# Hybrid backbone on one core: gate strips ahead of turnings, square sums by token, and inverse blocks copied by two engines

## The chip, the cores and the metric

One core of one Trainium2 chip. The metric is the device time of one execution in microseconds (us); the runs of the kernel before are three, with their median. TensorE is called PE below, VectorE DVE, ScalarE ACT, GpSimd POOL, and SyncE SP, as the profile does. "Granted clock" is the share of PE's full clock that it was given in a stretch: 1.00 is 2.4 GHz, 0.50 is 1.2 GHz.

## The reference, cut to what matters

Two layers over 256 latent tokens and 256 context tokens, 1024 channels, all float32. In each layer three branches (a short convolution, a two-directional recurrence over tokens, windowed attention) start from one modulated norm and are merged under sigmoid gates; a convolutional FFN follows. The context tokens are not needed after the last layer, so that the second layer computes only half of the token columns in most places.

```python
def rmsnorm(x, g):
    return x * lax.rsqrt(jnp.mean(x * x, axis=-1, keepdims=True) + NORM_EPS) * g

def modulate(x, g, shift, scale):
    return rmsnorm(x, g) * (1.0 + scale) + shift

def trunk_layer(xc, xl, c, c_ctx, cos, sin, p, ctx_out):
    hl, hc = modulate(xl, norm1_g, ...), modulate(xc, norm1_g, ...)
    # columns of h @ w_in: B, C, x of the convolution; r, k, v; three low-rank inputs; q, k, v; three gates
    att = windowed_attention(rope(q) * ATT_SCALE, rope(k), v, kc, vc, sink)   # context: context_attention
    # recurrence, forward and backward in t, 16 heads of 64:
    #   S = S * w_t + (S a_t) b_t^T + v_t k_t^T ;  y_t = S r_t
    rwkv = ((group_norm(y) * ln_g + ln_b) + bonus) * g
    conv = B * dwconv3(C * x, conv_w)
    m = sig(ga) * (conv @ a_out_w) + sig(gb) * (rwkv @ rwkv_out_w) + sig(gc) * (att @ attn_out_w)
    xl = xl + mod[2] * (m @ w_o)
    xl = xl + mod[5] * conv_ffn(modulate(xl, norm2_g, mod[3], mod[4]), p)
# the end: rmsnorm(xl, final_norm_g)
```

## The kernel before, in words

The activations lie with channels on the 128 partitions and the 512 tokens (256 context, 256 latent) along the free axis: xT and hT are 8 tiles of 128x512. Weights come in strips of 8 x 128x128 (512 KB) through a ring of 5 buffers that SP loads in the order in which PE uses them; a buffer comes free with the first matmul of the next strip. A strip is 8 matmuls of 512 columns (256 in the second layer where only the latent tokens count) into one PSUM bank; each of them is two entries of the trace, so that a strip is x16.

Every engine runs a stream of its own, written out by hand in program order, and waits on semaphores. PSUM is dealt out by three rings of two: A (banks 0, 1, small products that ACT copies out), G (6, 7, dense strips) and Q (pairs from 2 and 4, evacuated by DVE for the most part). `take` waits until the ring's next bank is free.

**The start** (`begin`): x and ctx are transposed on PE (L541), DVE copies them into xT (L1654) and squares them (L1605); 8 matmuls with a matrix of ones (`square_sum`, L486) sum the squares over channels and give every partition the sum of each token; ACT takes Ln and Exp (L1247, L1249), DVE multiplies (L1611). Beside that the modulation vectors come from four units of `ada_w` of 2 MB each (L496, copied by ACT at L1263, picked by PE at L518), and with them ACT modulates hT (L1257) for the first strips (L472). The same `square_sum` stands at the end of `merged_out` and of `ffn` in both layers: five norms, 8 matmuls each.

**Mixing** (`mix`, first loop over i, 8 passes per layer): one pass handles two heads, i.e. 128 channels. Its small matrix work stands between fillings: `fill(steps, n)` issues dense matmuls of the next pass's strips (order r, k, C, x, v, B) worth n halves of 256 columns. The order on PE in a pass is: `diagonal_blocks` (L606), `turn_hats`, `turn_values`, `pair_products`, a fill, `half_step` (L656, waits for DVE's chain from `turn_blocks` to `spread_blocks`, L1854 to L1914), `corners`, `below_left`, `value_products`, `corner_below`, `bonus_sums`, then for the next pass `key_sums` and `decays` (L590, L593), then `through_inverse` (L724, four blocks lrb0 to lrb3 from ring A, which ACT copies at L1392 after its own `decays`, L1325 and L1331), then the chain of 8 chunks `state_in` (L741) and `state_out` (L755) with a fill after each, and `outputs` (L773, L780). `state_out(0)` waits for `first_ready`, which DVE gives with `state_in(0)` (L1937). Between the chunks DVE computes the next pass's hats in small steps (L1762 to L1805); the fifth step (L1785) needs the exponentials that ACT makes in `powers` (L1339). ACT's copy of C is L1400 (`conv_gate`); the bank after it in ring G is wanted by the x strip.

**Attention** (`attend`, 8 steps t): scores on PE, maxima on DVE, exponentials on ACT, shares on DVE, then PE transposes the probabilities (`turn_probs`, L849), ACT copies them (L1447, L1450), and PE multiplies with the values (`weighted`, L861, copied at L1455). The gates and the output strips of the first two branches (`gate`, `branch`) are spread between. In the first layer a group of modulation columns is computed too (`ada_group` L506, `ada_pick` L518). All small products take ring A.

## Time and profile before

| | |
|---|---|
| runs | 3131.89, 3135.42, 3133.84 us; median 3133.84 |
| profiled execution | 3132.01 us, of which the span is 3130.2 |
| mean granted clock of PE | 0.973 |
| busy in the span | PE 2926.4, PE weight load 1763.4, DVE 1267.4, ACT 749.0, POOL 51.5 us |
| DMA | 264 MB, mean 84 GB/s |

The stretches of the span: start 0 to 75 us, mixing of the first layer to about 865, its attention to about 1290, the merge and FFN to about 1930, mixing of the second layer to about 2560, its attention, merge and FFN to the end. A row of a timeline gives start, duration, engine, line and operation, and in brackets how long the engine had been idle before it and who released it. Entries of PE overlap a little, so starts are what to compare.

### The profile page before, as it was taken

What the parts mean: (1) busy time and instruction counts of PE and PEld (TensorE: products, weight loads), DVE (VectorE), ACT (ScalarE), POOL (GpSimd) and SP (SyncE); (2) the same over time, 40 slices, a digit from 0 to 9 for tenths busy, and PEclk for the clock granted to TensorE, in tenths of its full rate; (3) what the DMA queues carried; (4) which work ended last, traced back from release to release, by engine and by line L of the source; (5) the groups of instructions that cost most, each with busy time, mean ns of one, the idle gap of its engine ahead of it and who ended that gap; (6) DMA issues with size and microseconds to landing.
All of it is one profiled execution on the core that took longest, in us unless ns stands there. A gap on an engine that the chain in (4) does not pass through costs nothing.

```text
span 3130.2 us, 57225 instructions
## 1 busy us (share of the span) xinstructions
PE 2926.4 (93%) x25233; PEld 1763.4 (56%) x25233; DVE 1267.4 (40%) x2564; ACT 749.0 (24%) x1456; POOL 51.5 (2%) x77
## 2 busy tenths in 40 slices
PE   7899999999989988999999999888998899999999
PEld 3455555555644444444444444555666667788887
DVE  2555555555222222112444211555666643322541
ACT  2233333233222112101111001323344422221110
POOL 1000000000000000000000000000000000000000
PEclk9999999999999998999999999989999999999999
DMA  7212222221324223322222223322211114344553
GB/s 232 71 42 65 71 58 65 72 65 50 82 74 106 77 78 91 88 74 66 78 74 81 69 74 102 85 64 72 72 52 45 45 44 122 108 115 129 158 150 115
DMA packets 499846, 264.26 MB, mean 84 GB/s; under 512 B 42848, under 2 KB 493744, under 8 KB 499088
## 3 DMA queue, kind: packets, MB, share of 16 engines
q1 hardware_dynamic: 497872, 251.57, 28.4%
q0 software_dynamic: 1728, 9.03, 0.8%
q8 instruction: 201, 3.29, 0.4%
q14 instruction: 45, 0.37, 0.0%
HBM read 255.31 MB, written 5.24 MB: 83 GB/s over the span
## 4 chain that ended last, share of the span: by engine, by line
PE 87%; ACT 6%; DVE 3%; issue 2%; DMA 2%; SPq 0%; DVEq 0%; ACTq 0%
PE psum L451 56%; PE psum L1018 7%; PE psum L472 2%; PE psum L638 2%; DMA strips<-in_w_in_dram 1%; PE psum L724 1%; PE psum L741 1%; ACT arena L1325 1%; PE psum L755 1%; PE psum L706 1%; PE psum L791 1%; PE psum L839 1%; PE psum L486 1%; PE psum L861 1%; PE psum L518 1%
## 5 line engine op out<-in xcount | busy, mean ns | idle before, releaser
L451 PE MATMUL psum<-hT,strips 128*128 128x512 f32 (+1 forms) x3968 | 1471.1, 520 | 48.6 <-ACT arena L1400 27.6
L451 PEld LDWEIGHTS psum<-hT,strips 128*128 128x128 f32 x3968 | 742.7, 194 | 576.9 <-issue 485.8
L1018 PE MATMUL psum<-arena,strips 128*128 128x512 f32 (+1 forms) x704 | 229.4, 486 | 0.0
L1018 PEld LDWEIGHTS psum<-arena,strips 128*128 128x128 f32 x704 | 133.7, 190 | 92.8 <-issue 83.5
L451 PE MATMUL psum<-arena,strips 128*128 128x512 f32 (+1 forms) x512 | 169.6, 486 | 3.0 <-DVE done L2058 3.0
L451 PEld LDWEIGHTS psum<-arena,strips 128*128 128x128 f32 x512 | 97.1, 190 | 71.5 <-issue 60.7
L2023 DVE SCALAR_TENSOR_TENSOR arena<-arena,psum 128x512 f32<-128x512 f32 (+1 forms) x32 | 17.7, 554 | 292.8 <-PE psum L451 292.8
L1556 ACT COPY arena<-psum 128x512 f32<-128x512 f32 (+1 forms) x88 | 42.1, 479 | 390.2 <-PE psum L451 375.4
L1673 DVE TENSOR_SCALAR arena<-arena 128x512 f32<-128x512 f32 (+1 forms) x88 | 37.0, 421 | 240.3 <-ACT arena L1556 240.1
L1835 DVE TENSOR_TENSOR arena<-psum,tables 128x1024 f32<-128x1024 f32 x48 | 58.5, 1220 | 110.3 <-PE psum L638 110.3
L724 PE MATMUL psum<-arena 64*64 64x128 f32 (+1 forms) x1024 | 67.8, 283 | 29.8 <-ACT arena L1331 25.5
L2171 DVE SCALAR_TENSOR_TENSOR arena<-psum,mod,arena 128x256 f32<-128x256 f32 x24 | 10.9, 481 | 208.6 <-PE psum L1018 208.6
L1435 ACT ACTIVATE arena<-psum,arena 128x512 f32<-128x512 f32 (+1 forms) x96 | 58.1, 613 | 149.1 <-DVE arena L1998 148.6
L1941 DVE TENSOR_TENSOR arena<-psum,arena 64x256 f32<-64x256 f32 x112 | 47.3, 422 | 109.9 <-PE psum L741 109.8
L1247 ACT ACTIVATE arena<-psum,tables 128x512 f32<-128x512 f32 (+1 forms) x5 | 3.0, 602 | 367.9 <-PE psum L486 367.9
L472 PE MATMUL psum<-hT,strips 128*128 128x512 f32 (+1 forms) x160 | 73.9, 626 | 16.4 <-ACT hT L1257 16.4
L451 PE MATMUL psum<-conv_branch,strips 128*128 128x512 f32 (+1 forms) x256 | 86.4, 490 | 1.9 <-ACT arena L1462 1.6
L1462 ACT ACTIVATE arena<-psum 128x512 f32<-128x512 f32 (+1 forms) x48 | 23.7, 495 | 267.4 <-PE psum L451 267.4
L451 PE MATMUL psum<-rwkv_branch,strips 128*128 128x512 f32 (+1 forms) x256 | 85.2, 486 | 0.0
L724 PEld LDWEIGHTS psum<-arena 64*64 64x64 f32 x1024 | 56.5, 146 | 45.3 <-ACT arena L1331 28.1
L638 PE MATMUL psum<-arena 64*128 64x128 f32 (+1 forms) x1024 | 75.3, 290 | 6.9 <-issue 6.9
L741 PEld LDWEIGHTS psum<-arena 64*64 64x64 f32 x896 | 35.0, 134 | 67.3 <-issue 49.0
(240 smaller groups left out, 3318.2 us busy)
## 6 DMA issues: line engine op xcount, KB each, us to landing
strips<-in_w_in_dram SPq DMA_DIRECT2D x158, 512.0 KB, 4.2
strips<-in_ffn_up_dram SPq DMA_DIRECT2D x88, 512.0 KB, 3.8
strips<-in_ada_w_dram SPq DMA_DIRECT2D x80, 512.0 KB, 3.8
strips<-in_ffn_down_dram SPq DMA_DIRECT2D x32, 512.0 KB, 4.0
arena<-in_ada_w_dram SPq DMA_DIRECT2D x4, 2048.0 KB, 15.3
strips<-in_w_in_dram SPq DMA_DIRECT2D x32, 256.0 KB, 3.8
strips<-in_a_out_w_dram SPq DMA_DIRECT2D x16, 512.0 KB, 4.5
strips<-in_rwkv_out_w_dram SPq DMA_DIRECT2D x16, 512.0 KB, 5.8
```

The source lines that it names most:

```text
L451: ins = mm(s.o[:, first:T], strip[:, b, k, :], rhs[:, k, first:T], k == 0, k == KT - 1)
L472: ins = mm(ss[j].o[:, first:T], strip[:, bs[j], k, :], hT[:, k, first:T], k == 0, k == KT - 1)
L486: ins = mm(s.o[:, lo:T], ones[:, :], sq[:, k, lo:T], k == 0, k == KT - 1)
L638: ins = one(PS[:, b0 + h, (c % 4) * n:(c % 4 + 1) * n], BK[d][rows(h), c].rearrange("p j t -> p (j t)"), ar[d][rows(h), c, 0:n // CH].rear ...
L724: ins = one(PS[r, BANK_A[s.b], q * n:(q + 1) * n].rearrange("p (k t) -> p k t", t=CH), TLR[r, 8 * h + 4 * d + m].rearrange("p b t -> p (b ...
L741: ins = one(PS[r, BANK_P[s.b] + h, d * CH:(d + 1) * CH], AR[i % 2][d][rows(h), c, 0, :], GG[rows(h), c, d, :])
L1018: ins = mm(s.o[:, lo:T], strip[:, b, j, :], hid[:, k, lo:T], k == 0, k == FT - 1)
L1435: ins = act.activation(pr[u][:, x:x + 2 * T // g], PS[:, b0 + x // T, x % T:x % T + 2 * T // g], ACT.Exp, bias=st[:, u, 1, i:i + 1], accum ...
L1556: act.copy(upp[:, b, lo // SEG:, 1:SEG + 1], s.o[:, lo:T].rearrange("p (s t) -> p s t", t=SEG)).then_inc(s.free, 1)
L1673: ts(dst, src[:, :, 1:n + 1], g1, None, MUL).then_inc(s_vec, 1)
L1835: tt(EE[:, 0:2, j, d].rearrange("p k h c t -> p k (h c) t").rearrange("p k q t -> p q k t"), o, mask.unsqueeze(1).broadcast_to([P, 8, 2, C ...
L1941: tt(dst, o, add, ADD).then_inc(s.free, 1)
```

## The change

- `gate(0, t)` goes ahead of `turn_probs(t, 2)`, and `gate(1, t)` ahead of `turn_probs(t, 0)`, on PE and ACT; `ada_pick` of attention goes behind `branch(0, t)`.
- For the first norm ACT squares the rows of x token by token with an accumulated sum, takes Ln and Exp on 4 columns, DVE spreads each over 128 columns, and PE turns these 4 tiles (`spread_tokens`). For the four others DVE adds the first 7 squares up and PE multiplies two tiles with the ones instead of 8.
- In mixing, DVE copies lrb0 and lrb1, placed between its `bonus` and its `decays`, ACT only lrb2 and lrb3. ACT's `conv_gate(i + 1)` goes ahead of its `through_inverse`. PE fills 4 (2 in the second layer) between `decays(i + 1)` and `through_inverse`, and a little less between the chunks. `diagonal_blocks(i + 1)` goes ahead of `outputs(i)`. `ada_pick` goes behind a fill. DVE's `conv_taps` goes ahead of its last `state_in`.

```diff
-            def square_sum(n, k, lo):
+            def square_sum(n, lo, last):
-                if k == 0:
+                if not last:
                     take(A, "norm", n)
                 s = slots["norm", n]
-                pe.wait_ge(ev["sq_ready"], KT * n + k + 1)
-                ins = mm(s.o[:, lo:T], ones[:, :], sq[:, k, lo:T], k == 0, k == KT - 1)
-                if k == KT - 1:
+                pe.wait_ge(ev["sq_ready"], 2 * n + last - 1)
+                ins = mm(s.o[:, lo:T], ones[:, :], sq[:, KT - 1 if last else 0, lo:T], not last, last)
+                if last:
                     ins.then_inc(s.full[0], 1)
+            def spread_tokens():
+                pe.wait_ge(ev["rows_ready"], 1)
+                s = take(A, "norm", 0)
+                for j in range(4):
+                    ins = one(s.o[:, j * P:(j + 1) * P], rs_rows[:, j, :], tab["ident"])
+                ins.then_inc(s.full[0], 1)
...
                         if t > 0:
                             weighted(t - 1, 1)
+                        gate(0, t)
                         if lo == 0:
                             turn_probs(t, 2)
-                        if t > 0 and ATT_ADA[l][t - 1]:
-                            ada_pick(A, *ATT_ADA[l][t - 1], part_att)
-                        gate(0, t)
...
                         branch(0, t)
+                        if t > 0 and ATT_ADA[l][t - 1]:
+                            ada_pick(A, *ATT_ADA[l][t - 1], part_att)
                         scores(t, 1)
                         if lo == 0:
                             weighted(t, 0)
+                        gate(1, t)
                         turn_probs(t, 0)
-                        gate(1, t)
...
                 fill(steps, everything)
+                diagonal_blocks(0)
                 for i in range(KT):
                     ahead = i < KT - 1
                     steps = dense(i + 1) if ahead else attention_dense()
-                    diagonal_blocks(i)
...
                     half_step(i)
+                    pair_products(1, 0, i)
+                    fill(steps, 10 if wide else 6)
                     if MIX_ADA[l][i]:
                         ada_pick(A, *MIX_ADA[l][i], part_mix)
-                    pair_products(1, 0, i)
-                    fill(steps, 10 if wide else 6)
...
                         decays(i + 1)
+                        fill(steps, 4 if wide else 2)
                     through_inverse(i, ahead)
...
-                            fill(steps, 4 if wide else 2.4)
+                            fill(steps, 3.8 if wide else 2.3)
...
                     fill(steps, everything)
+                    if ahead:
+                        diagonal_blocks(i + 1)
                     outputs(i)
```

ACT: the start, and a pass of mixing.

```diff
-                norm(0, 0)
+                act.wait_ge(s_x, 64)
+                for j in range(4):
+                    ins = act.activation(hT[:, 2 * j:2 * j + 2, :].rearrange("p k t -> p (k t)"), xin[:, j, :], ACT.Square,
+                                         accum_out=token_rs[:, j:j + 1])
+                ins.then_inc(s_act, 1)
+                act.wait_ge(*order.next())
+                act.activation(token_rs, token_rs, ACT.Ln, bias=tab["eps_norm"], scale=1.0 / D).then_inc(s_act, 1)
+                act.wait_ge(*order.next())
+                act.activation(token_rs, token_rs, ACT.Exp, scale=-0.5).then_inc(ev["token_ready"], 1)
+                s = await_slot("norm", 0)
+                act.copy(rs, s.o).then_inc(ev["rs_ready"], 1)
...
                 def through_inverse(i):
-                    for m in range(4):
+                    for m in range(2, 4):
...
                         decays(i + 1)
+                        conv_gate(i + 1)
                     through_inverse(i)
                     if ahead:
                         powers(0, i + 1)
-                        conv_gate(i + 1)
                         powers(1, i + 1)
```

DVE: the squares, the start, and a pass of mixing.

```diff
             def square(k, lo):
-                tt(sq[:, k, lo:T], xT[:, k, lo:T], xT[:, k, lo:T], MUL).then_inc(ev["sq_ready"], 1)
+                ins = tt(sq[:, k, lo:T], xT[:, k, lo:T], xT[:, k, lo:T], MUL)
+                if k == KT - 1:
+                    ins.then_inc(ev["sq_ready"], 1)
+                elif k > 0:
+                    ins.then_inc(s_vec, 1)
+                    dve.wait_ge(*order.next())
+                    ins = tt(sq[:, 0, lo:T], sq[:, 0, lo:T], sq[:, k, lo:T], ADD)
...
+                dve.wait_ge(ev["token_ready"], 1)
+                for j in range(4):
+                    ins = ts(rs_rows[:, j, :], ones[:, :], token_rs[:, j:j + 1], None, MUL)
+                ins.then_inc(ev["rows_ready"], 1)
...
+                def through_inverse(i):
+                    for m in range(2):
+                        s = filled(f"lrb{m}", i)
+                        k0 = 1 if 2 * m >= c0 else 2
+                        n = (3 - k0) * 4 * CH
+                        for p in range(2):
+                            r = rows(p)
+                            ins = dve.tensor_copy(EE[r, k0:3, m // 2, :, :, 2 * (m % 2) + p].rearrange("p k d h t -> p k (d h) t").rearrange("p k q t -> p q k t"),
+                                                  PS[r, BANK_A[s.b], 0:n].rearrange("p (q k t) -> p q k t", q=4, t=CH))
+                        ins.then_inc(s.free, 1)
...
                     bonus(i)
+                    through_inverse(i)
                     if ahead:
                         decays(i + 1)
...
+                        if ahead and c == NCH - 2:
+                            t = conv_taps(i + 1)
                     if ahead:
-                        t = conv_taps(i + 1)
```

## Rows read from the trace of the kernel before

**Rows 1.** The page: busy time by engine (us, share, instructions), and the chain.

```profile
PE 2926.4 (93%) x25233; PEld 1763.4 (56%) x25233; DVE 1267.4 (40%) x2564; ACT 749.0 (24%) x1456; POOL 51.5 (2%) x77
...
PE 87%; ACT 6%; DVE 3%; issue 2%; DMA 2%; SPq 0%; DVEq 0%; ACTq 0%
```

**Rows 2.** PE's waits from 880 to 1330 us: total us, times, longest.

```profile
PE psum L849 <- ACT arena L1455: 19.9, 8, 2.5
PE psum L518 <- ACT arena L1447: 12.8, 7, 3.0
...
PE psum L849 <- DVE arena L2011: 3.0, 2, 1.5
```

**Rows 3.** Timeline of PE in the first layer's attention, t = 2 to 3.

```profile
1024.11 1.02 PE L518 MATMUL psum<-tables,arena 128*128 128x2 f32 x8 [1.35 <-ACT arena L1447]
1025.00 8.81 PE L451 MATMUL psum<-hT,strips 128*128 128x512 f32 x16
...
1047.27 7.03 PE L451 MATMUL psum<-hT,strips 128*128 128x512 f32 x16
```

**Rows 4.** Windows: length, busy by engine, granted clock, DMA share, GB/s.

```profile
860.00:1290.00 430.00, 384.22 (x1704) 187.08 (x1703) 99.05 (x244) 87.42 (x245) 0.00 (x0) 0.96 0.32 86
```

**Rows 5.** Timeline of PE in the first layer's mixing, pass 3.

```profile
452.13 2.14 PE L724 MATMUL psum<-arena 64*64 64x128 f32 x32 [1.51 <-ACT arena L1331]
...
455.52 0.45 PE L755 MATMUL psum<-arena 128*64 128x64 f32 x8
...
460.85 1.98 PE L451 MATMUL psum<-hT,strips 128*128 128x512 f32 x4 [0.29 <-ACT arena L1400]
```

**Rows 6.** Timeline of DVE in the same pass.

```profile
437.99 0.68 DVE L1924 COPY arena<-psum 32x512 f32<-32x512 f32 x1 [3.67 <-PE psum L683]
...
450.48 0.69 DVE L1749 TENSOR_SCALAR arena<-arena 128x1024 f32<-128x1024 f32 x1 [5.70 <-ACT arena L1325]
...
452.25 2.33 DVE L1754 TENSOR_TENSOR_SCAN arena<-tables,arena 128x512 f32<-128x512 f32 x2
454.50 0.26 DVE L1937 COPY arena<-arena 64x256 f32<-64x256 f32 x1
...
458.77 0.69 DVE L1785 SCALAR_TENSOR_TENSOR arena<-arena 128x512 f32<-128x512 f32 x1
```

**Rows 7.** Timeline of ACT in the same pass.

```profile
451.95 4.89 ACT L1392 COPY arena<-psum 64x512 f32<-64x512 f32 x8
456.86 0.64 ACT L1339 ACTIVATE arena<-arena 128x512 f32<-128x512 f32 x1
...
460.21 0.58 ACT L1400 COPY arena<-psum 128x512 f32<-128x512 f32 x1 [1.96 <-PE psum L451]
```

**Rows 8.** Timeline of PE in the second layer's mixing, pass 5.

```profile
2400.28 1.29 PE L656 MATMUL psum<-arena 32*32 32x32 f32 x128 [1.49 <-DVE arena L1914]
...
2426.20 2.62 PE L724 MATMUL psum<-arena 64*64 64x64 f32 x48 [2.13 <-ACT arena L1331]
...
2432.20 0.70 PE L451 MATMUL psum<-hT,strips 128*128 128x256 f32 x2 [1.59 <-ACT arena L1400]
```

**Rows 9.** Line L486, all its instructions: min/median/max ns, first and last start.

```profile
L486 PE MATMUL psum<-hT,ones x80: 379/592/697, 21.2 to 3119.7; 128*128 128x512 f32 x48, 128*128 128x256 f32 x32
```

**Rows 10.** Timeline of PE and DVE at the start.

```profile
12.30 4.38 PE L541 MATMUL psum<-tables,arena 128*128 128x128 f32 x24 [5.39 <-DMA arena<-in_x_dram]
...
15.57 1.29 DVE L1605 TENSOR_TENSOR hT<-arena 128x512 f32<-128x512 f32 x2
...
21.18 7.13 PE L486 MATMUL psum<-hT,ones 128*128 128x512 f32 x16
...
39.56 11.98 PE L472 MATMUL psum<-hT,strips 128*128 128x512 f32 x24 [1.74 <-ACT hT L1257]
```

**Rows 11.** Line L1088, the loads of the four ada units.

```profile
L1088 SPq DMA_DIRECT2D arena<-in_ada_w_dram x4: 639/1646/3748, 4.2 to 27.6; - x4
...
DMA to landing us min/median/max: 10.6/15.3/20.9
```

More of the change, by code:

```diff
@@ L544, in begin @@
                 turn_params(0)
-                for k in range(KT):
-                    square_sum(0, k, 0)
+                spread_tokens()
                 pe.wait_ge(ev["c_ready"], 1)
@@ L987, in mix @@
                         if c > 0:
-                            fill(steps, 4 if wide else 2.4)
+                            fill(steps, 3.8 if wide else 2.3)
                         if c < NCH - 1:
                             state_out(c, i)
-                            fill(steps, 4 if wide else 2.4)
+                            fill(steps, 3.8 if wide else 2.3)
                     fill(steps, everything)
+                    if ahead:
+                        diagonal_blocks(i + 1)
                     outputs(i)
@@ L1194, in load_params @@
                 if l == 0:
-                    pool.memset(ones[:, :], 1.0)
                     for m in range(DEPTH):
@@ L1477, in attend @@
                         exps(t, 0)
+                        gate(0, t)
                         if lo == 0:
@@ L1481, in attend @@
                             ada_raw(*ATT_ADA[l][t - 1])
-                        gate(0, t)
                         exps(t, 1)
@@ L1485, in attend @@
                             weighted(t, 0)
+                        gate(1, t)
                         probs(t, 0)
-                        gate(1, t)
                         if ATT_ADA[l][t]:
@@ L1604, in square @@
             def square(k, lo):
-                tt(sq[:, k, lo:T], xT[:, k, lo:T], xT[:, k, lo:T], MUL).then_inc(ev["sq_ready"], 1)
+                ins = tt(sq[:, k, lo:T], xT[:, k, lo:T], xT[:, k, lo:T], MUL)
[5 more added lines that the diff above has]
+                    ins = tt(sq[:, 0, lo:T], sq[:, 0, lo:T], sq[:, k, lo:T], ADD)
+                    if k == KT - 2:
+                        ins.then_inc(ev["sq_ready"], 1)
+                    else:
+                        ins.then_inc(s_vec, 1)
+                        dve.wait_ge(*order.next())
             def scaled(n, lo):
@@ L1644, in begin @@
             def begin():
+                dve.memset(ones[:, :], 1.0).then_inc(s_vec, 1)
+                dve.wait_ge(*order.next())
                 s = await_slot("c")
@@ L1654, in begin @@
                     dve.tensor_copy(xT[:, 2 * u:2 * u + 2, :], PS[:, BANK_P[s.b]:BANK_P[s.b] + 2, :]).then_inc(s.free, 1)
-                    dve.wait_ge(*s.freed)
-                    for k in range(2 * u, 2 * u + 2):
-                        square(k, 0)
+                dve.wait_ge(ev["token_ready"], 1)
+                for j in range(4):
+                    ins = ts(rs_rows[:, j, :], ones[:, :], token_rs[:, j:j + 1], None, MUL)
+                ins.then_inc(ev["rows_ready"], 1)
                 setup(0)
```

17 lines of the change are left out of this document (9 added, 8 removed).

## The prediction, made before the changed kernel was run

> **What bounds the kernel now.** I read the page first: PE is busy 93% of the span and is 87% of the chain that ended last [rows 1]. So time is won where PE stands idle, where its clock is low, or where it has less to do; work moved from ACT to DVE wins nothing by itself. Then I asked for PE's waits stretch by stretch, since the average hides that they differ. In the first layer's attention 35.7 us are waits for small copies and shares, in three kinds [rows 2]: 19.9 in 8 (one per step, the second half of `turn_probs(t, 0)` waits until ACT has come to a copy queued behind exponentials), 12.8 in 7 (`ada_pick` behind `turn_probs(t, 2)`), 3.0 in 2. The same stretch shows a granted clock of 0.96, that is 0.04 x 430 = 17 us lost [rows 4]. The strip behind such a wait shows the second loss: 8.81 us, where the same strip without it takes 7.03 [rows 3]; each fall of the clock costs about 1.8 us. Then I read one pass of mixing in each layer on PE, DVE and ACT side by side [rows 5 to 8]. The first layer's passes are nearly full: 1.51 and 0.29 us of waits in a pass of some 91. The second layer's have 2.13, 1.59 and, in the passes without an ada group, 1.49.
>
> **Attention.** Before each of the two turnings there now stands a gate strip, 7.0 us of PE work [rows 3] that needs nothing but its weights. The wait of 2.49 goes: ACT's queued copies take about 1.5 us. `ada_pick` has a whole `branch` strip between it and the turning. The ring sees the same order of strips. All 35.7 us go. For waits that go the clock stays up: I take 14 of the 17 us, since waits for strips behind each ada group stay. Next late there is nothing that I can find: the copy of the gate is hidden by the turning that follows it. Sum: -50. Bounds: -36 if the clock keeps falling for the waits that stay, -53 at most. In the second layer these turnings show no waits; 0.
>
> **Square sums.** 80 entries are 40 matmuls [rows 9]. The 16 entries of one wide norm take 7.13 us [rows 10], so 0.86 us a matmul after the overlap, half of it with 256 columns. Four norms lose 6 matmuls each: 2 x 6 x 0.86 + 2 x 6 x 0.43 = 15.5 us, all on PE between strips. DVE gets 6 additions per norm of about 0.65 us (the squares: 1.29 for two [rows 10]) while PE's next strip takes 7.0 (or 3.5): hidden. The end of a norm is as long as before: then too, two products stood behind the last strip. Sum: -15.5; bounds -12 (if a wait takes part of it) and -16.
>
> **The start.** x is there at 12.3 us [rows 10]. ACT squares 4 tiles of 128x1024; 512 columns cost it about 0.6 [rows 7], so 1.1 each: 16.8. Ln, a table load and Exp on 4 columns: about 19.8 at most with two table loads of some 1.3. DVE, freed of its squares, has xT by 19.5; 4 small spreads, PE's four turnings, ACT's copy: rs at about 22, where before the sums alone end at 28.3 [rows 10]. Then another bound takes over: the units of `ada_w`. The second one, issued near 5, lands 20.9 us later [rows 11], at 25.9; its product, copy and pick, and the first modulated tile, took 32.7 to 39.6 before, some 6.9 us that start at 25.9 now. So the first strip starts near 32.6 in place of 39.6 [rows 10]: -7. Bounds: -10 (this stretch ran in part at the low clock) and -3 (the low clock lies across more of it). The second half of the start keeps its order, and its loads have time. ones on DVE costs 0.2 us before anything is due.
>
> **Mixing, first layer.** Here I expect a loss. Before, DVE starts `decays` at 450.48, as soon as ACT has given it data, and gives `first_ready` at 454.8 (0.69, 0.69, 2.33 and 0.26 us [rows 6]), a little before PE comes to `state_out(0)` at 455.52 [rows 5]. Now two copies per block stand ahead of `decays` in DVE's queue, and they wait for PE. In this pass's times: PE ends `decays` at 449.5 (lrb1 starts at 452.13 behind a wait of 1.51 and lrb0's 1.1 [rows 5]), fills 1.95 us (half of the x16 strip's half), and does lrb0 from 451.5 to 452.5 and lrb1 to 453.6; the wait of 1.51 is gone. DVE copies two halves of lrb0 and two of lrb1 at 0.65 each: 452.6 to 455.2; lrb2 and lrb3 wait 0.35 and 0.3 for these and end at 456.3. `decays` then takes DVE to 458.8, `state_in(0)` to 459.1. PE stands idle 459.1 - 456.3 = 2.8 us. Behind PE's wait is everything, since `state_out(0)` is next in its queue and no fill is ahead of it. The second wait is on ACT: 22 matmuls of fill are issued before `through_inverse`, and C is complete with the 24th. So `conv_gate`, now first, waits for the fill behind `state_out(0)`, 2.35 us after its start; then it takes 0.6, two blocks take 4.89 / 2 = 2.4 [rows 7], and the first `powers` 1.4 (456.86 to 458.3). They are ready 6.8 us after `state_out(0)` starts; before, they were ready ahead of DVE's fifth step at 458.77 [rows 6]. DVE stands there, with `state_out(1)` behind it in its queue, and PE reaches `state_in(2)` 1.5 us before that is done. The wait of the x strip for C (0.29) stays. Idle per pass: 0.65 + 2.8 + 1.5 + 0.3 = 5.2, against 2.0 before (with 0.2 at lrb3): +3.2 a pass, 7 passes, +22. A stall of 2.8 us within a few us of others lets the clock fall in perhaps half of the passes, 1.8 each less what it costs there now: +5. Sum +27. Bounds: +8 (DVE's copies at the rate of its small 64-row copy of 0.26, ACT ahead) and +38 (a clock fall in each pass). Earlier `diagonal_blocks` bring DVE's chain forward by the outputs, 3.8 us, but `half_step` does not wait for it in this layer in most passes: 0. Its cover if DVE were later: the fill of 7 us ahead of it. The moved `ada_pick` is hidden both ways.
>
> **Who should copy from PSUM** is a point where the Trainium skill speaks against this change. DVE's copy of 512 columns from PSUM is 0.68 to 0.70 [rows 6], ACT's 4.89 / 8 = 0.61 [rows 7]. The Trainium skill (VectorE: DVE Perf Modes, Specifications) puts it that ScalarE sits closer to PSUM and VectorE closer to SBUF; the rows agree, by 0.08 us a copy. By that alone the change would cost 4 x 0.08 = 0.3 us a pass at the one place where DVE is late. In my sum it is not the rate but the place in DVE's queue that costs.
>
> **Mixing, second layer.** The same steps with blocks half as large: the fill is 2 halves, which completes C, so that `conv_gate` does not wait and the 1.59 goes. lrb1 still waits 1.1 for ACT's copy of g in place of 2.13 [rows 8]. PE has lrb1 at 2426.9, DVE's two copies of it (about 0.4 each with 256 columns) end at 2427.75, `decays` and `state_in(0)` need the 3.8 us of [rows 6]: 2431.5. PE, waiting 0.3 for lrb1's bank, is done with lrb3 at 2429.1: 2.4 of idle. 3.5 in place of 4.0 us: -0.5 a pass. `half_step`'s 1.49 [rows 8] shrinks only by 0.65, since DVE's chain, brought forward by 2 us, meets `masked_pairs`, whose products PE makes no earlier; this for four passes. With the last pass of each layer, where two engines share the copies and nothing else is late (-1 each): -3.5 - 2.6 - 2 = -8. I keep 3 of it back for the clock: -5. Bounds -15 and +10, by whether the stall of 2.4 brings the clock down.
>
> **The sum** against the profiled execution: 3132.0 - 50 - 15.5 - 7 + 27 - 5 = 3081.5; its time is 1.8 below the median of the runs, so 3083.
>
> **Rivals.**
> (a) The mixing doesn't lose: DVE's place is covered, because `first_ready` was given earlier than I think or the copies are short. For it: DVE was idle 5.70 us ahead of `decays` [rows 6]. Against it: it was idle before PE has lrb0. Mixing 0 in place of +27: 3056.
> (b) The mixing loses more: a clock fall in every pass of both layers and `state_in` late more than once per pass. +27 becomes +40, -5 becomes +10: 3111.
> (c) The gates only move the wait: if a gate strip is not there in time, PE waits for its load where it waited for a copy. The ring is emptied by four ada strips in 2 us, and PE waits for strips already. If half of attention's gain goes so: 3108.
> (d) Slower than before: DVE never catches up in the chain of chunks. A pass has 7 links from DVE to PE; if each came late, at 1 us a link, 14 passes are +98 on top of the rest, 3180. It decides from where DVE's work between two links exceeds PE's time for them, 4.7 us in the first layer (two fills of 1.98 and two small products) and 3.3 in the second. DVE's is about 3.8 in both while hats are computed, for four of the seven links, so that in the second layer it is close.
>
> **Chances.** My sum 0.48; (a) 0.20; (b) 0.17; (c) 0.11; (d) 0.04. The forecast is that of the likeliest, 3083. Its own range by the bounds is 3068 to 3098; to hold 8 in 10 it must take in most of (a) and of (b) and (c): 3054 to 3110. A measurement of this kernel can tell about 0.2%, 6 us, from no change. Within it lies only what is between (b) and (d), 0.02; slower 0.03; faster 0.95.
>
> **What would show it.** Right: in attention no wait at L849 and L518, waits for strips unchanged, a clock near 0.99; L486 with 16 entries in the four later norms; the first strip near 32.6 with the wait ahead of it on the second unit. In the first layer's mixing a wait of `state_out(0)` near 2.8 for DVE's `first_ready`, one of `state_in(2)` near 1.5, none for g. Wrong: `state_out(0)` without a wait would take the +27 away; waits at each chunk in the second layer would mean (d).

## The result, and the profile after

The changed kernel takes 3108.8 us (median of 4 runs, 3100.3 to 3118.2) against 3132.9 of the kernel before (4 runs): ratio 0.9922, 95% interval 0.9894 to 0.995. It is faster by 24 us, where 50 were forecast. The time lies in the range, but the gain is less than half of the forecast, and most of the reason is in one stage.

The page of the profiled execution (span 3116.4 us, the slowest of the four runs) answers to [rows 1]; it shows next to nothing, 18 us less of PE's work and 44 us more of DVE's:

```profile
PE 2908.8 (93%) x25177; PEld 1757.7 (56%) x25177; DVE 1311.2 (42%) x2649; ACT 724.3 (23%) x1401; POOL 51.6 (2%) x76
```

So the span has to be cut by stage. The marks are events that both traces have: the first dense strip, ACT's square of the last pass in mixing, ACT's Ln in each norm. Lengths in us, of one profiled execution each:

| stage | before | after | difference | forecast |
|---|---|---|---|---|
| start, to the first dense strip | 73.8 | 65.1 | -8.7 | -7 |
| mixing, first layer | 776.3 | 834.2 | **+57.9** | +27 |
| attention and merge, first layer | 604.9 | 542.2 | **-62.7** | -55 |
| FFN, first layer | 469.8 | 465.2 | -4.6 | -5 |
| mixing, second layer | 683.7 | 692.0 | +8.3 | -5 |
| attention and merge, second layer | 274.1 | 272.3 | -1.8 | -2.6 |
| FFN, second layer, and end | 247.6 | 245.3 | -2.3 | -2.6 |

The differences sum to -13.8 us and not to -24, because the profiled execution of the changed kernel is the slowest of its four. Its granted clock is 0.970 over a span of 3116.4 us; the fastest has 0.975 and 3098.5 us, and 0.005 x 3116 is some 16 of the 18 us between them. So the same kernel varies by that much through the clock alone, and a stage rich in clock falls, as mixing is, can hold several us of it.

The windows of the two changed stages, before and after (columns as in [rows 4]). Before:

```profile
73.80:850.10 776.30, 733.02 (x10057) 426.25 (x10055) 414.31 (x739) 249.66 (x410) 16.27 (x18) 0.98 0.23 62
850.10:1455.10 605.00, 557.42 (x2111) 262.96 (x2110) 125.88 (x295) 100.37 (x270) 3.12 (x7) 0.97 0.31 86
```

After:

```profile
65.10:899.30 834.20, 753.97 (x10057) 437.53 (x10055) 435.17 (x771) 231.86 (x378) 16.57 (x18) 0.95 0.21 58
899.30:1441.60 542.30, 530.71 (x2098) 254.87 (x2098) 130.12 (x301) 99.56 (x270) 3.12 (x7) 1.00 0.35 95
```

Both stages moved in idle time and in clock. Mixing has the same 10057 entries of PE as before, but is busy 754 us with them instead of 733, at a clock of 0.95 instead of 0.98, and idle 80 instead of 43. Attention is idle 12 us instead of 48, at a clock of 1.00.

PE's waits in attention of the first layer: of [rows 2] none is left. The largest is that of the strips behind the ada groups (8.4 us in 6 before); beside it stand only two single waits of 1.7 and 0.8 us:

```profile
PE psum L453 <- DMA strips<-in_w_in_dram: 8.8, 6, 2.5
```

PE's waits in the first layer's mixing (line, whom it waited for: total us, times, longest), after:

```profile
PE psum L764 <- DVE arena L1983: 18.6, 7, 2.7
PE psum L680 <- issue: 9.6, 4, 2.8
PE psum L453 <- DVE arena L1847: 8.8, 7, 1.3
PE psum L750 <- DVE arena L1998: 8.6, 7, 1.4
PE psum L453 <- ACT arena L1420: 8.2, 5, 7.1
PE psum L733 <- DVE arena L1973: 7.6, 16, 0.6
PE psum L624 <- ACT arena L1432: 4.1, 7, 0.6
```

Line numbers have moved: L764 is `state_out`, L1983 the copy that gives `first_ready`, L750 `state_in`, L733 `through_inverse` and L1973 DVE's copies in it, L453 a dense strip, L1847 `gated`, L624 `turn_hats`, L1432 ACT's copy of y. The wait of 1.51 for g at [rows 5] is gone from this list. The 7.1 in the fifth line is in the prologue and stood there before.

The same pass as in [rows 5 to 7], after. PE:

```profile
460.20 1.88 PE L453 MATMUL psum<-hT,strips 128*128 128x512 f32 x4
462.01 1.97 PE L733 MATMUL psum<-arena 64*64 64x128 f32 x32
464.60 1.09 PE L733 MATMUL psum<-arena 64*64 64x128 f32 x16 [0.61 <-DVE arena L1973]
466.02 1.09 PE L733 MATMUL psum<-arena 64*64 64x128 f32 x16 [0.33 <-DVE arena L1973]
469.77 0.69 PE L764 MATMUL psum<-arena 128*64 128x64 f32 x8 [2.66 <-DVE arena L1983]
470.39 3.78 PE L453 MATMUL psum<-hT,strips 128*128 128x512 f32 x4
```

DVE:

```profile
463.15 2.81 DVE L1973 COPY arena<-psum 64x512 f32<-64x512 f32 x4 [7.60 <-PE psum L733]
466.00 0.69 DVE L1784 TENSOR_SCALAR arena<-arena 128x1024 f32<-128x1024 f32 x1
466.61 0.69 DVE L1786 TENSOR_SCALAR arena<-arena 128x1024 f32<-128x1024 f32 x1
467.21 2.33 DVE L1789 TENSOR_TENSOR_SCAN arena<-tables,arena 128x512 f32<-128x512 f32 x2
469.46 0.26 DVE L1983 COPY arena<-arena 64x256 f32<-64x256 f32 x1
...
478.51 0.69 DVE L1820 SCALAR_TENSOR_TENSOR arena<-arena 128x512 f32<-128x512 f32 x1 [3.24 <-ACT arena L1362]
```

Read it downwards. DVE stands idle for 7.60 us. In the last 1.9 us of them the input of its `decays` is there (ACT's L1345, L1325 before, starts at 459.96, and DVE could follow 1.28 us later, as it did before), but its copies come first in its queue and wait for PE. Then copies, `decays` and the copy for `first_ready` run without a gap from 463.15 to 469.7, and PE waits for the last of them. The strip behind takes 3.78 us for four entries that take 1.98 elsewhere; the clock there is half. Two windows of 2 us behind the stall (466 to 468 still shows 1.00; in this pass the clock falls at 469.2, 0.6 us before the stall ends):

```profile
470.00:472.00 2.00, 2.00 (x10) 1.11 (x9) 1.90 (x5) 0.00 (x0) 0.00 (x0) 0.50 0.00 0
472.00:474.00 2.00, 2.00 (x3) 0.34 (x1) 0.54 (x1) 0.00 (x0) 0.00 (x0) 0.50 0.00 0
```

### The profile page after: what moved, and what is told of

It reads as the page before. It is cut to its first block, busy times and chain, and to the rows that moved or that the text cites. A ratio compares the mean times of both kernels' runs of the same rounds, so it can differ in the third digit from the quotient of the medians.

```text
span 3116.4 us, 57161 instructions
## 1 busy us (share of the span) xinstructions
PE 2908.8 (93%) x25177; PEld 1757.7 (56%) x25177; DVE 1311.2 (42%) x2649; ACT 724.3 (23%) x1401; POOL 51.6 (2%) x76
## 4 chain that ended last, share of the span: by engine, by line
PE 87%; DVE 5%; ACT 4%; issue 2%; DMA 2%; SPq 0%; DVEq 0%; ACTq 0%
PE psum L453 55%; PE psum L1028 7%; PE psum L474 2%; PE psum L647 2%; DMA strips<-in_w_in_dram 1%; PE psum L750 1%; PE psum L764 1%; PE psum L870 1%; DVE arena L1789 1%; PE psum L848 1%; PE psum L800 1%; PE psum L715 1%; PE psum L637 1%; PE psum L858 1%; DVE arena L1973 1%
## 5 line engine op out<-in xcount | busy, mean ns | idle before, releaser
L453 PE MATMUL psum<-hT,strips 128*128 128x512 f32 (+1 forms) x3968 | 1483.3, 523 | 46.4 <-DMA strips<-in_w_in_dram 20.5
L453 PEld LDWEIGHTS psum<-hT,strips 128*128 128x128 f32 x3968 | 747.0, 195 | 580.5 <-issue 491.5
L453 PE MATMUL psum<-arena,strips 128*128 128x512 f32 (+1 forms) x512 | 167.9, 486 | 3.0 <-DVE done L2104 3.0
L453 PEld LDWEIGHTS psum<-arena,strips 128*128 128x128 f32 x512 | 97.1, 190 | 71.5 <-issue 60.7
L764 PEld LDWEIGHTS psum<-arena 128*64 128x64 f32 x896 | 35.7, 138 | 102.4 <-DVE arena L1983 40.6
L764 PE MATMUL psum<-arena 128*64 128x64 f32 x896 | 51.4, 237 | 37.3 <-DVE arena L1983 37.3
L453 PE MATMUL psum<-conv_branch,strips 128*128 128x512 f32 (+1 forms) x256 | 85.8, 488 | 0.3
L453 PE MATMUL psum<-rwkv_branch,strips 128*128 128x512 f32 (+1 forms) x256 | 85.2, 486 | 0.0
L750 PEld LDWEIGHTS psum<-arena 64*64 64x64 f32 x896 | 36.8, 140 | 82.2 <-issue 42.5
L1973 DVE COPY arena<-psum 64x512 f32<-64x512 f32 (+1 forms) x64 | 35.5, 555 | 101.9 <-PE psum L733 101.2
```

The lines of the kernel that those rows point to most:

```text
L453: ins = mm(s.o[:, first:T], strip[:, b, k, :], rhs[:, k, first:T], k == 0, k == KT - 1)
L750: ins = one(PS[r, BANK_P[s.b] + h, d * CH:(d + 1) * CH], AR[i % 2][d][rows(h), c, 0, :], GG[rows(h), c, d, :])
L764: ins = one(PS[rows(h), BANK_P[s.b], d * CH:(d + 1) * CH], EE[:, 2, c // 4, d, h, c % 4, :], RV[:, c, d, h, :])
L1973: ins = dve.tensor_copy(EE[r, k0:3, m // 2, :, :, 2 * (m % 2) + p].rearrange("p k d h t -> p k (d h) t").rearrange("p k q t -> p q k t"), ...
```

## The experiments

All ratios are to the kernel before, run beside the kernel in question on the same chip. It took 3132.9 us beside the changed kernel, 3134.5 beside e1 to e4, 3129.8 beside e5 to e8 and 3129.1 beside e9 to e12; across these groups the ratios compare better than the times. The two stages are those of one profiled execution each.

| kernel | us | ratio, 95% interval | mixing, first layer | mixing, second layer |
|---|---|---|---|---|
| changed kernel | 3108.8 | 0.9922, 0.9894 to 0.9950 | 834.2 | 692.0 |
| e1 mixing as before | 3057.4 | 0.9751, 0.9733 to 0.9768 | 777.4 | 684.7 |
| e2 ACT copies all | 3066.8 | 0.9782, 0.9768 to 0.9797 | 787.4 | 686.0 |
| e3 DVE copies behind decays | 3101.3 | 0.9891, 0.9876 to 0.9906 | 821.5 | 687.5 |
| e4 diagonal behind outputs | 3102.1 | 0.9891, 0.9874 to 0.9908 | 824.8 | 691.9 |
| e5 e2, gated early | 3063.5 | 0.9782, 0.9760 to 0.9804 | 779.3 | 688.9 |
| e6 DVE copies the last two | 3068.4 | 0.9801, 0.9783 to 0.9819 | 783.8 | 688.6 |
| e7 C copy at old place | 3093.2 | 0.9879, 0.9855 to 0.9902 | 816.7 | 683.0 |
| e8 e5, diagonal late | 3050.3 | 0.9745, 0.9721 to 0.9768 | 773.3 | 686.3 |
| e9 fill behind the blocks | 3084.4 | 0.9855, 0.9839 to 0.9871 | 811.2 | 680.8 |
| e10 gates alone | 3070.4 | 0.9810, 0.9793 to 0.9827 | 776.2 | 683.1 |
| e11 sums and start alone | 3119.7 | 0.9965, 0.9947 to 0.9983 | 782.1 | 680.0 |
| e12 e1 with DVE's copies | 3106.8 | 0.9926, 0.9907 to 0.9945 | 811.3 | 702.8 |

The second layer's mixing differs by up to 5 us between kernels whose code there is the same (before, e1, e10, e11: 680.0 to 684.7), the first layer's by 6. Differences of that size in one column say nothing.

**e1: everything but mixing.**

```diff
@@ the changed kernel, all edits of mixing undone @@
-                        fill(steps, 4 if wide else 2)
...
-                    if ahead:
-                        diagonal_blocks(i + 1)
...
-                    for m in range(2, 4):
+                    for m in range(4):
...
-                    through_inverse(i)
                     if ahead:
                         decays(i + 1)
```

> The changed kernel with all six edits of mixing undone (copies, place of the C copy, fills, diagonal blocks, the pick, conv_taps); the gates, the square sums and the start stay changed. Theory: by stages of the two traces, mixing costs the change 57.9 us in the first layer and 8.3 in the second, and everything else gives 80. So this kernel should stand at 3133 - 80 = 3053 us, with the first layer's attention as short as in the changed kernel (542 against 605 us to the next norm). Rival: attention is short only because mixing hands over its buffers in another state, and its gain goes with mixing: 3090 or above.

3057.4 us (some 3053 expected), attention and merge of the first layer 542.9. The rival falls: all of the loss is in mixing, and it takes 50 us from a kernel that has 77 to give.

**e2: ACT copies all four blocks.**

```diff
-                    for m in range(2, 4):
+                    for m in range(4):
...
-                        conv_gate(i + 1)
                     through_inverse(i)
                     if ahead:
                         powers(0, i + 1)
+                        conv_gate(i + 1)
...
-                    through_inverse(i)
                     if ahead:
                         decays(i + 1)
```

> The changed kernel with all four inverse blocks copied by ACT and the C copy at its old place (ahead of the copies it would wait for itself); the fill ahead of through_inverse, the early diagonal blocks, the pick and conv_taps stay. Theory A (DVE's place in its queue): the waits for first_ready (2.66 each, 14) and for state_in(2) (up to 1.4) and for DVE's copies vanish and with them two clock falls of 1.7 per pass of the first layer: 7 passes x 8 = 56 and some 20 in the second layer, and the wait for g (1.5, 2.1) stays gone by the fill: near 3035. Theory B (too many small products in a row, diagonal blocks beside outputs, starve PE of instructions and pull the clock down): most of the loss stays: near 3080.

3066.8: the copies, with the C copy that goes with them, are 42 us, most of the loss, but not all; theory B falls as the main cause, and theory A was too generous. PE's waits in the first layer's mixing now:

```profile
PE psum L453 <- ACT arena L1420: 11.7, 8, 7.1
PE psum L680 <- issue: 10.0, 4, 3.0
PE psum L453 <- DVE arena L1847: 8.8, 7, 1.3
PE psum L624 <- ACT arena L1432: 4.1, 7, 0.6
```

The waits for `first_ready`, for `state_in(2)` and for g are gone. Two are left that the kernel before does not have and that the prediction's sum (the "blind sum" of the expectations) does not have either: 8.8 us in 7 of a strip for DVE's `gated`, and 4.1 in 7 of `turn_hats` for ACT's copy of y. In the second layer a strip waits for C, 18.6 us in 7, where the kernel before had 11.2 in 7, since ACT comes to it later:

```profile
PE psum L453 <- ACT arena L1420: 18.6, 7, 2.7
```

**e3: the copies behind decays.**

```diff
                     bonus(i)
-                    through_inverse(i)
                     if ahead:
                         decays(i + 1)
+                    through_inverse(i)
```

> The changed kernel with DVE's two copies behind its decays instead of ahead of them. Theory A (what costs is that decays and first_ready wait behind copies that wait for PE): DVE does decays while PE fills, copies lrb0 and lrb1 at about +2 us of where they are now; lrb2 and lrb3 wait 2 us in all, but state_out(0) waits little: 1 to 1.5 us less per pass and fewer clock falls in it: 3085 to 3095. If the place does not matter, only the number of copies on DVE: 3109, unchanged.

3101.3, outside of what theory A gave by 6. It is 7.5 below the changed kernel, with intervals that overlap; the profiled stage is shorter by 12.7. The wait moves from L764 to L733, which now shows 20.8 us in 12, up to 2.7 each, in the first layer. At the head of the pass DVE's queue has no good place: either the copies hold `decays`, or `decays` holds the copies, and PE needs both before `state_out(0)`.

**e4: the diagonal blocks back at the head of the pass.**

```diff
-                    if ahead:
-                        diagonal_blocks(i + 1)
                     outputs(i)
```

> The changed kernel with the diagonal blocks back at the head of the pass, behind the outputs. Theory A: they cover ACT's copy of y again (0.8 us a pass in the first layer, 0.2 in the second), but DVE's chain starts 2 to 4 us later, so that half_step waits 0.5 longer in the second layer: within 6 us of 3109. Theory B (small products in a row): some 20 us faster, 3089, with the waits of PE that nothing explains (issue) back to half.

3102.1, 6.7 below the changed kernel, with intervals that overlap. The wait of `turn_hats` for y is gone (4.1 us), `half_step` in the second layer waits 5.2 instead of 2.9, and the waits that nothing explains are nearly as long as in the changed kernel (20.0 us in the first layer, where it has 21.7). Theory B has no case in this layer's waits; a small gain is left that the runs cannot separate from none.

**e5: gated earlier.**

```diff
-                            if ahead:
-                                gated(i + 1)
...
+                        if ahead and c == 4:
+                            gated(i + 1)
```

> As e2 (ACT copies all four blocks), and DVE's product for the x strip (gated) is placed behind its state_out(4) instead of behind state_in(5). Theory: the new wait of a dense strip for that product (8.8 us in 7, first layer) comes from the fill drawn ahead of through_inverse, which brings the B strip two matmuls forward; with gated early it vanishes, and a clock fall in each pass with it: 9 to 20 us less than e2's 3067, i.e. 3047 to 3058. Rival: the strip's place is not the cause of e2's remaining loss against e1 (10 us), which lies in the diagonal blocks: 3064 or more.

The wait of 8.8 us is gone from the list, as expected, and the first layer's mixing is shorter by 8.1. But 3063.5 is outside the 3047 to 3058 that were expected, and the ratio is e2's, 0.9782, so over the whole kernel the gain is not shown; the stage loses as much to the clock as e2's (22 us, where e2 has 20), so that the second half of the theory, a clock fall saved in each pass, does not hold; the second layer was 3 us longer in this profile.

**e6: DVE copies two blocks, but the last two.**

```diff
-                    for m in range(2):
+                    for m in range(2, 4):
...
-                    through_inverse(i)
                     if ahead:
                         decays(i + 1)
...
                             state_out(c, i)
+                            if c == 0:
+                                through_inverse(i)
```

> DVE still copies two of the four inverse blocks, but the last two (lrb2, lrb3), and behind its state_out(0); ACT copies the first two; the C copy is back at its old place. Theory (the place in DVE's queue costs, not the copying itself): decays and first_ready are not held up, the chain needs these blocks only at chunk 4, so the waits for first_ready vanish and the time is near e2's, 3067, at most 1.4 us a pass in the first layer above it: 3060 to 3080. Rival (DVE has no room for 2.5 us more in any place of the pass): 3095 to 3110, with waits of PE for state_in or state_out at the first chunks.

3068.4: the same number of copies on the same engine, and 38 us less than the changed kernel by the ratios; of these the place of the C copy accounts for some 14 (e7), so that against e7, which has it at the same place and ran beside it, 25 are left. The first layer's waits for `first_ready` are 2.1 us in all:

```profile
PE psum L764 <- DVE arena L1987: 2.1, 7, 0.3
```

So it is not the number of copies on DVE that costs. e6 changes two things at once, the place in the queue and which blocks DVE copies, and both belong to the gain: lrb2 and lrb3 are needed late, while lrb0 and lrb1 hold the banks that lrb2 and lrb3 wait for. With lrb0 and lrb1 behind `decays` little was won (e3). In the second layer, where a chunk is shorter, even this place is late: `state_out(1)` waits 2.4 in each of 7 passes for DVE's `state_in`, 16.9 us.

**e7: ACT's copy of C at its old place.**

```diff
                         decays(i + 1)
-                        conv_gate(i + 1)
                     through_inverse(i)
                     if ahead:
                         powers(0, i + 1)
+                        conv_gate(i + 1)
```

> The changed kernel with only ACT's copy of C back behind the first powers. Theory: the wait of state_in(2) (1.2 to 1.4 us in 7 passes of the first layer, 8.6 in all) comes from ACT holding its block copies and powers behind an unfinished C; it vanishes here, but in the second layer the x strip may wait for C again: 3096 to 3104 against 3109. Rival: state_in(2) is late because DVE's decays are late: the wait stays, 3109.

3093.2, 16 below the changed kernel (14 by the ratios, whose intervals just overlap) and 3 below what was expected; in the profiles the first layer's mixing is 17.5 us shorter. The wait of `state_in(2)` is gone from the list (8.6 us in 7), that of `first_ready` is unchanged:

```profile
PE psum L764 <- DVE arena L1983: 18.6, 7, 2.7
PE psum L680 <- issue: 9.9, 4, 3.1
PE psum L453 <- DVE arena L1847: 8.8, 7, 1.3
```

**e8: what is best of it.**

```diff
@@ e5, and @@
-                    if ahead:
-                        diagonal_blocks(i + 1)
                     outputs(i)
```

(The pick is back ahead of its fill as well.)

> As e5, with the diagonal blocks back behind outputs and the pick back: what is left of the change in mixing is the fill ahead of through_inverse, conv_taps and the early gated. Theory: the fill hides the wait for g (10.6 us in the first layer, 14.9 in the second before), the diagonal blocks are worth what half_step waits in the second layer less what turn_hats waits for y: within 6 us of e5, and below e1's 3057: 3035 to 3055. Rival: the clock takes back what waits give: 3057, as e1.

3050.3, the fastest of all: 13 us below e5 measured beside it, with intervals that just touch, and not to be told from e1 by its ratio. The fill ahead of the blocks takes the wait for g away (10.6 us in e1's first layer), and mixing is 773.3 where e1 has 777.4. In the second layer the wait for C is 18.6 us in 7, as in e2. Whether it is faster than e1 is not settled.

**e9: the fill where the stall is.**

```diff
-                        fill(steps, 4 if wide else 2)
                     through_inverse(i, ahead)
+                    if ahead:
+                        fill(steps, 4 if wide else 2)
```

> The changed kernel with the new fill (4, or 2 in the second layer) behind PE's through_inverse, directly ahead of state_out(0), instead of ahead of through_inverse. The wait for g (1.5) comes back and the wait of 2.66 for first_ready shrinks by the 1.95 us of fill, to about 0.9: the sum of waits in a pass stays within 0.5 us. Theory: the long stall is what lets the clock fall there (two falls of 1.7 in a pass behind it), so that cutting it in two short waits gives back 1.7 or more per pass of the first layer: 3085 to 3098. Rival: the clock follows the sum of idle time: 3105 to 3110.

3084.4, 24 below the changed kernel (21 by the ratios, whose intervals are apart). One pass, PE:

```profile
455.51 1.96 PE L733 MATMUL psum<-arena 64*64 64x128 f32 x32 [1.51 <-ACT arena L1352]
458.09 1.09 PE L733 MATMUL psum<-arena 64*64 64x128 f32 x16 [0.62 <-DVE arena L1974]
459.11 1.98 PE L453 MATMUL psum<-hT,strips 128*128 128x512 f32 x4
461.84 0.45 PE L764 MATMUL psum<-arena 128*64 128x64 f32 x8 [0.75 <-DVE arena L1984]
462.23 1.98 PE L453 MATMUL psum<-hT,strips 128*128 128x512 f32 x4
```

and the stage:

```profile
67.20:878.40 811.20, 737.52 (x10057) 429.23 (x10056) 435.08 (x771) 231.87 (x378) 16.28 (x18) 0.98 0.22 60
```

The waits of the pass are 1.51, 0.62 and 0.75 where the changed kernel has 0.61, 0.33 and 2.66: 0.7 us less, 5 in the stage. But PE is busy 737.5 us with the same 10057 entries, 16.5 less than in the changed kernel, at a clock of 0.98 instead of 0.95, and the strip behind `state_out(0)` takes 1.98. None of the falls of this stage lies behind `state_out(0)`. So the one long stall cost the fall of the clock there, and nearly the same waiting in pieces did not. How much of the 16.5 us is the stall's is less sure, since the changed kernel's profile is of its slowest run; the comparison over all kernels below does not hang on it.

**e10: the gates alone**, on the kernel before (on ACT in the same way, and the other gate too).

```diff
+                        gate(0, t)
                         if lo == 0:
                             turn_probs(t, 2)
-                        if t > 0 and ATT_ADA[l][t - 1]:
-                            ada_pick(A, *ATT_ADA[l][t - 1], part_att)
-                        gate(0, t)
```

> The kernel before with only the order of attention changed (gates ahead of the turnings, ada_pick behind the branch). From the stages: first layer's attention with its merge was 604.9 us and is 542.2, of which 5 are square sums: -57 to -58, so 3076. My blind sum had -50, 3083.

3070.4, ratio 0.981: 59 us, the stage 544.7 against 604.9. The waits of [rows 2] are gone here too, and the waits for strips are 7.1 us in 6.

**e11: sums and start alone**, on the kernel before.

```diff
-                for k in range(KT):
-                    square_sum(0, k, 0)
+                spread_tokens()
...
-                square_sum(2 * l + 2, KT - 1, lo)
+                square_sum(2 * l + 2, lo, False)
+                square_sum(2 * l + 2, lo, True)
```

> The kernel before with only the square sums and the start changed. Blind sum -15.5 and -7: 3110. From the stages: start -6 to -10, the four norms -5, -4.6, -1.8 and -2.3 = -14: 3108 to 3114.

3119.7, ratio 0.9965: 5 to 17 us, where the prediction's sum had 22.5 and the stages led me to expect some 20. The stages that hold little else show the forecast gains: start 67.0 (-6.8), FFN of the first layer 463.9 (-5.9), attention and merge of the second 271.9 (-2.2). The first layer's mixing and attention, whose code is unchanged up to the five sums, were 5.8 and 3.0 longer in this profile, the latter at a clock of 0.96. So the gain is there by stage, and over the whole kernel some 9 us of it are not seen in these runs, most of them within what two equal stages differ by.

**e12: the copies alone**, on e1.

```diff
-                    for m in range(4):
+                    for m in range(2, 4):
...
                     bonus(i)
+                    through_inverse(i)
                     if ahead:
                         decays(i + 1)
```

> The kernel e1 (gates, sums and start changed, mixing as before) with one edit of mixing added: DVE copies the first two inverse blocks, ahead of its decays. No fill, no early C, no early diagonal blocks. Theory: first_ready comes 2.7 to 2.9 us late in each of 14 passes beside the wait for g, which stays, and the clock falls behind it: waits +3.1 and clock +1.7 to +3.4 a pass in the first layer, some +1 to +3 in the second: 3057 + 34 to 50, i.e. 3090 to 3107. Rival: the copies cost only together with the other edits, which take their cover: 3057 to 3070.

3106.8 against e1's 3057.4 (ratios 0.9926 and 0.9751): this one edit costs 49 us by the times, 55 by the ratios, by itself. PE's waits in the first layer's mixing:

```profile
PE psum L764 <- DVE arena L1980: 18.6, 7, 2.7
PE psum L733 <- ACT arena L1348: 10.6, 7, 1.5
```

The first layer's stall is the same 2.66 to the hundredth, with and without fill, early C and early diagonal blocks. In the second layer it is 14.1 us in 7, and the stage is longest there, 702.8. The other edits of mixing, put on top of this one, make the changed kernel as a whole neither better nor worse than e12. By stage they cost in the first layer (834.2 against 811.3), where the fill wins 10.6 us at g and 21.5 are lost at `state_in(2)`, at `gated` and at y, and give some of it back in the second (692.0 against 702.8).

## Why the prediction was right and wrong, step by step

**What bounds the kernel: right.** Nearly every gain and loss is PE's idle time or PE's clock; the rest is the work of the square sums that PE no longer does, and 5 us in attention that are open. ACT gave 25 us of work away, and no gain of its own came of it.

**Attention: right, 8 short.** -58 without the sums (and -59 in e10) against -50, beyond my bound of -53. The waits went whole: 36 of the 58 are idle time (605.0 - 557.4 before, 542.3 - 530.7 after). The clock term was 3 too small: I kept back 3 of 17 us for the waits for strips that stay, but those (8.8 us) let it fall once; the stage now shows 1.00, and 17 us fewer are lost to the clock. The other 5 are busy time that neither the sums nor the granted clock explains; e10, which has no other edit, shows the same 5. What they are is open.

**Square sums: right by stage.** The four later norms have 16 entries in all, where they had 64 [rows 9], and the stages that hold little beside them lost 4.6, 1.8 and 2.3 us, where 5, 2.6 and 2.6 were forecast. In e11 alone the whole kernel gained less than the sum.

**Start: the number right, the bound wrong.** -8.7, in other profiles -6 to -9 (-10 in e8), against -7. The first modulated strip starts at 32.07, where 32.6 was forecast. But the bound that I named, the second unit's load, is not seen: PE was never waiting for it. The product of the first unit took 3.32 us from 21.65, at the low clock, and that with copy and pick brought PE to the second unit at 26.64, 0.7 us behind my landing time. From there to the strip it took 5.4 us and not 6.9, since the low clock now lay on the first unit's product and no longer on the second's (1.92 us, where it took 3.38 before). The two errors cancel, so part of this hit is luck.

**Mixing, first layer: the step that failed.** The mechanism was right and so were its terms one by one, in the row's own numbers: `first_ready` 2.66 (forecast 2.8), `state_in(2)` 1.2 to 1.4 (1.5), the blocks 0.94 (0.65), g gone. DVE's four copies took 2.81 us, 0.70 each, where the estimate was 0.65; ACT's take 0.59 here, so that the remark on the two engines stands, though of the rows it named for DVE only the 0.68 reads PSUM. The steps that failed are the clock term, taken at 5 us, and two waits that the sum put at nothing. What was missing, 31 us:

- The clock, 21 us more of busy time where I had 5. I took a fall in half of the passes, from the attention rows, where I had seen a stall of 2.49 without a fall and one of 1.35 with it. Not every stall of 2.49 is harmless: in the kernel before, three of the eight are followed by a fall, and four of the five of 1.35. That is seven of thirteen, so that half was fair for attention; it did not carry over to mixing. Two of the 2.49, the first with a slow strip behind it, the second with the strip of 7.03 us at 1047.27 in [rows 3]:

```profile
881.03 0.66 PE L849 MATMUL psum<-tables,arena 128*128 128x128 f32 x4 [2.49 <-ACT arena L1455]
881.52 8.73 PE L451 MATMUL psum<-hT,strips 128*128 128x512 f32 x16
...
1046.77 0.66 PE L849 MATMUL psum<-tables,arena 128*128 128x128 f32 x4 [2.49 <-ACT arena L1455]
```

  The stall of 2.66 with 0.94 ahead of it brings the clock down in six of the seven passes, in two of them for twice as long (3.4 us at half the clock, or 6.8), which makes 13.6 us; in e4, e7 and e12, with the same stall, it does so in 18 of 21. The whole stage loses 39 us to the clock, where it lost 15 before; the other 10 of this growth lie elsewhere in the passes, and why is open. That the stall is the cause is shown by e9, and by all kernels together: the five whose first layer has a stall of 2.7 us in each pass, at `state_out(0)` or at the blocks ahead of it (the changed kernel, e3, e4, e7, e12), have a granted clock of 0.95 to 0.96 in this stage, the nine others 0.97 to 0.98.
- `gated`, 8.8 us: the fill drawn ahead of the blocks brings the B strip two matmuls forward, and its bank is given free by `gated`, which DVE does only behind `state_in(5)`. I followed C through the moved fill and not the strips behind it. Shown by e5, where the wait is gone.
- ACT's copy of y, 4.1 us: the diagonal blocks stood between `outputs` and `turn_hats` and covered it. I asked what the moved blocks wait for, and not what they had hidden. Shown by e4 and e8, where it is gone.
- About 5 us more of waits that the profile calls issue; what they come from is open.

**Mixing, second layer: the waits right, the sum wrong**, +8.3 for -5. `first_ready` 2.66 (2.4), g 1.27 (1.1), C gone (as said), `half_step` 2.9 us in 3 passes for 4.3 in 3. The stall of 2.66 costs 18.6 us and the other three changes (g, C, `half_step`) give 18.6 back; on top, what is idle in all grew by 3 and busy time, i.e. clock, by 5. Part of it may be nothing: kernels with the same code here differ by 5 us.

**The rivals.** (b), a clock fall in every pass, is what happened, for the first layer as a mechanism: it had 0.17. Its second half, `state_in` late more than once per pass, did not happen. That its 3111 is so near the 3108.8 is luck: it gave mixing +50 where the profiles have +66, and the other stages won more than forecast. (a) is refuted by the wait of 2.66 itself and by e12, (c) by the strips' waits, (d) too: DVE catches up after `state_in(2)`, and in the changed kernel no later chunk waits. I weighed (b) too low: I priced it as a matter of chance per stall, from stalls of other kinds in another stage.

## What to carry to other kernels

In an engine's in-order queue a moved piece costs by where it stands: two blocks on DVE cost some 50 us ahead of `decays`, where their copies wait for PE and hold up what PE needs next, and almost nothing where DVE took the two that are needed last and copied them behind the first chunk. When work is drawn ahead or moved, follow every bank and buffer that it advances, and ask of the moved work what it had covered. Put independent dense work where the stall is, not somewhere near it: the same fill behind the blocks instead of ahead of them was worth 21 to 24 us. And a rate of clock falls that was read in one stage did not hold in another: seven of thirteen stalls in attention, 24 of 28 in mixing.

## What the runs showed of the hardware

- The clock does not follow the sum of idle time. Waits of 0.61, 0.33 and 2.66 us in one pass were followed by 3.4 to 6.8 us at 1.2 GHz in six of seven passes, waits of 1.51, 0.62 and 0.75 in the same place in none; PE's busy time over the stage grew by 21 us against 5 us, compared with the kernel before. Of the waits of 2.49 us in the attention of the kernel before, five of eight were followed by strips at full speed, of those of 1.35 us only one of five. A stall's cost in clock cannot be read from its length alone.
- In attention, taking away 36 us of waits brought 58 us: 17 more came from the clock, which went from 0.97 to 1.00 over the stage, and 5 are open.
- Copying 64x512 from PSUM took DVE 0.70 us a piece (2.81 for 4) and ACT 0.59 (2.37 for 4). The Trainium skill (VectorE: DVE Perf Modes, Specifications) places ScalarE closer to PSUM, and the trace agrees; at 0.11 us a copy it is 0.4 us a pass and not what decided.
